# The S5 recurrence as one stage in four chunks: rotated inputs, a hardware scan, and GpSimd beside VectorE

## What is computed

```python
def s5_mixer(x, w_in, lam_re, lam_im, log_dt, b_re, b_im, c_re, c_im, d_skip, w_glu):
    ...
    u = (x @ w_in).astype(f32)
    ...
    a_bar = jnp.exp(lam * dt)
    b_bar = ((a_bar - 1.0) / lam)[..., None] * lax.complex(b_re.astype(f32), b_im.astype(f32))
    ...
        bu = jnp.einsum('gpc,btgc->btgp', b_bar, u_c.astype(jnp.complex64))
        _, hs = lax.associative_scan(binop, (jnp.broadcast_to(a_bar, bu.shape), bu), axis=1)
        hs = hs + a_pow[None] * h[:, None]
        y = jnp.einsum('gcp,btgp->btgc', c, hs).real
    ...
    y = jnp.moveaxis(ys, 0, 1).reshape(bsz, seq, D_MODEL) + d_skip.astype(f32) * u
    hid = jax.nn.gelu(y.astype(x.dtype), approximate=False)
    val, gate = jnp.split(hid @ w_glu, 2, axis=-1)
    return val * jax.nn.sigmoid(gate)
```

## Time and profile before

| | us |
|---|---|
| median of 3 runs | 2594.73 |
| lowest, highest | 2594.63, 2598.16 |
| span of the profiled execution, first to last instruction | 2590.5 |
| `s5_u`, from 836.3 to 886.3 | 50.0 |
| `s5_tables` to `s5_gelu`, from 886.3 to 981.0 | 94.7 |
| `s5_glu`, half clock at its start | 982.0 to 988.8 |

### The profile page before, as it was taken

The page is one execution under the profiler, slowest core; times in us unless marked ns, Lnnn a source line. Parts: engine busy times, 40 slices in busy tenths (PEclk is TensorE's granted clock), DMA queues, the critical chain, the costliest instruction groups (busy, mean ns, idle before and its releaser), DMA issues. The chain is left out here.

```text
span 2590.5 us, 41313 instructions
## 1 busy us (share of the span) xinstructions
PE 2477.6 (96%) x15961; PEld 2036.9 (79%) x15961; DVE 1739.2 (67%) x2869; ACT 1051.9 (41%) x1561; POOL 589.9 (23%) x447
## 2 busy tenths in 40 slices
PE   8998999999999989899999999998999999999998
PEld 6788887788887768899999999886776576767566
DVE  6945656467676784576666767676687567487667
ACT  4443233321212333355555555533344443344453
POOL 2404321430230020052333432440024001024001
PEclk9999999999999999999999999999999999999999
DMA  4321002346654252267776777853221211332121
GB/s 155 98 83 35 2 3 65 124 156 237 212 182 148 76 166 84 91 219 229 254 240 224 252 236 231 271 184 125 86 74 60 76 66 57 109 94 70 33 82 65
DMA packets 259968, 339.98 MB, mean 131 GB/s; under 512 B 24928, under 2 KB 217952, under 8 KB 259232
## 3 DMA queue, kind: packets, MB, share of 16 engines
q1 hardware_dynamic: 251840, 315.52, 37.6%
q0 software_dynamic: 4512, 15.99, 1.8%
q10 hardware_dynamic: 3456, 6.29, 0.8%
HBM read 318.63 MB, written 16.52 MB: 129 GB/s over the span
## 5 line engine op out<-in xcount | busy, mean ns | idle before, releaser
L3020 PE MATMUL ps<-x_feat_r,moe_w_hi 128*128 128x384 f32 x1408 | 405.1, 361 | 0.6 <-DVE x_feat_r L3132 0.6
L2545 DVE TENSOR_TENSOR moe_w_lo<-ring,moe_w_hi 128x2048 fp32r<-128x2048 f32 x144 | 316.1, 2196 | 126.8 <-ACT moe_w_hi L2540 126.6
L3023 PE MATMUL ps<-x_feat_r,moe_w_lo 128*128 128x192 f32 x1408 | 354.0, 251 | 0.0
L2540 ACT ACTIVATE moe_w_hi<-ring 128x2048 fp32r<-128x2048 f32 x144 | 254.8, 1770 | 93.5 <-PE ps L263 76.2
L3023 PEld LDWEIGHTS ps<-x_feat_r,moe_w_lo 128*128 128x128 f32 x1408 | 269.2, 191 | 0.3
L3020 PEld LDWEIGHTS ps<-x_feat_r,moe_w_hi 128*128 128x128 f32 x1408 | 264.3, 188 | 1.7 <-issue 1.4
L267 PE MATMUL ps<-x_free_r,ring_r 128*128 128x512 f32 x496 | 195.6, 394 | 0.0
L266 PE MATMUL ps<-ring_r,x_feat_r 128*128 128x256 f32 (+2 forms) x576 | 185.1, 321 | 0.0
L263 PE MATMUL ps<-x_feat_r,ffn_w_hi 128*128 128x512 f32 x352 | 139.3, 396 | 1.2 <-DVE ffn_w_lo L2488 1.2
L267 PE MATMUL ps<-x_feat_r,ffn_w_lo 128*128 128x512 f32 x352 | 139.4, 396 | 0.0
L266 PE MATMUL ps<-x_free_r,ffn_w_hi 128*128 128x512 f32 x352 | 138.5, 393 | 0.0
(11 more groups left out here) (661 smaller groups left out, 6407.1 us busy)
## 6 DMA issues: line engine op xcount, KB each, us to landing
ring<-in_moe_w SPq DMA_DIRECT2D x120, 1024.0 KB, 5.5
ring<-in_w_in SPq DMA_DIRECT2D x32, 1024.0 KB, 5.3
ring<-in_ffn_w SPq DMA_DIRECT2D x30, 1024.0 KB, 7.4
ring<-in_ada_t SPq DMA_DIRECT2D x48, 512.0 KB, 4.3
ring<-in_gdn_w_in SPq DMA_DIRECT2D x12, 1024.0 KB, 6.0
ring<-in_moe_w SPq DMA_DIRECT2D x24, 512.0 KB, 3.8
ring<-in_s_w_glu SPq DMA_DIRECT2D x8, 1024.0 KB, 5.6
ring<-in_w_out SPq DMA_DIRECT2D x8, 1024.0 KB, 6.2
```

What stands on the lines that cost most here:

```text
L2540: self.prog.nc.scalar.activation(self.flat(self.hi, j % SPLITS, j), self.raw(j), ACT.Copy).then_inc(self.hi_done, 1)
L2545: self.prog.nc.vector.tensor_tensor(self.flat(self.lo, j % SPLITS, j), self.raw(j), self.flat(self.hi, j % SPLITS, j).bitcast(F32), ALU.su ...
L3020: mm = nc.tensor.matmul(out, wh[:, k, cs], both[:, k, :], start=(k == 0), stop=False)
L3023: mm = nc.tensor.matmul(out[:, 0:SLOTS], wl[:, k, cs], xg[0][:, k, :], start=False, stop=(k == KD - 1))
```

## The change

Names first. `SC` = 4 chunks of `SQ` = 8 pairs. `S5Room` lays out the buffers: `u_ring` keeps only three feature blocks of u; `rot` holds cosine and sine of the angle of the pole's power for 63 steps, `decay` its magnitude.

- In `s5_u` GpSimd fills `rot` by doubling and `decay` by a broadcast copy (`rotations`): 36 products and sums, six for each of 32, 64, 128, 256, 512 and 992 elements in a partition. VectorE's own list there is the same as before.
- The four stages after it become one, `s5_core`. E stays in PSUM. For each chunk VectorE turns E by the angle (reading PSUM), runs `tensor_tensor_scan` with the real `decay` on the real and the imaginary part, multiplies by the cosine, and adds what GpSimd has made meanwhile: the two products by the sine (`cross`).
- The lags take b_bar widened to 32 columns (`lag_w`, which GpSimd fills), one matmul for both groups of a pair. The skip term is added to the lags (`add_skip`, GpSimd). `within` and `states` add up in the same PSUM banks, so VectorE's addition (L2366) and the skip operation (L2405) go.
- SyncE lays out each `mix` in 16 DMAs, in place of 8. After them it loads the four tiles of `s5_glu`, each when its chunk has been read.
- Of `keep_busy`, 14 matmuls stay in `s5_core`; before there were 16 in `s5_scan` and 18 in `s5_gelu`.

```diff
+def rotations(nc, link, s5, room):
+    tt = nc.gpsimd.tensor_tensor
+    rot, turn = room.rot, room.turn
+    nc.gpsimd.memset(rot[:, 0, :, 0], 1.0)
+    nc.gpsimd.memset(rot[:, 1, :, 0], 0.0)
+    for part in range(2):
+        nc.gpsimd.tensor_copy(rot[:, part, :, 1], s5.pole[:, 1 + part, :])
+    link(nc.gpsimd.tensor_copy(room.decay, s5.pole[:, 0, :].unsqueeze(2).to_broadcast([P, PAIRS, NJ])))
+    link(nc.gpsimd.memset(room.decay[:, :, 0], 0.0))
+    n = 1
+    while n < NJ - 1:
+        m = min(n, NJ - 1 - n)
+        shape = [P, PAIRS, m]
+        re, im = (rot[:, part, :, 1:m + 1] for part in range(2))
+        top_re, top_im = (rot[:, part, :, n:n + 1].to_broadcast(shape) for part in range(2))
+        t = [x[:, :, 0:m] for x in turn]
+        tt(t[0], re, top_re, ALU.mult)
+        tt(t[1], im, top_im, ALU.mult)
+        tt(t[2], re, top_im, ALU.mult)
+        link(tt(t[3], im, top_re, ALU.mult))
+        tt(rot[:, 0, :, n + 1:n + m + 1], t[0], t[1], ALU.subtract)
+        link(tt(rot[:, 1, :, n + 1:n + m + 1], t[2], t[3], ALU.add))
+        n += m
...
+        def u_feat(f):
+            return room.u_ring[:, f % room.U_RING]
...
+        @st.gpsimd
+        def _(pool):
+            rotations(nc, linker(pool, pool_link), s5, room)
...
+            turn_tables(0)
+            turn_tables(1)
+            inputs(0)
+            turn_tables(2)
+            turn_tables(3)
+            lags(0)
+            lags(1)
+            inputs(1)
+            lags(2)
+            lags(3)
+            within(0)
+            states(0)
+            inputs(2)
+            lags(4)
+            lags(5)
+            turn_back(0)
+            within(1)
+            states(1)
+            inputs(3)
+            lags(6)
+            lags(7)
+            turn_back(1)
+            within(2)
+            states(2)
+            turn_back(2)
+            within(3)
+            states(3)
+            pe.wait_ge(e_read, SC)
+            keep_busy(prog, E_BANK, 4)
+            turn_back(3)
+            keep_busy(prog, E_BANK, 10)
...
+            def scan(b):
+                e, t, h = room.e, room.t, room.h[b % 2]
+                shape = [P, 2, SQ, NJ]
+                cos, sin = (rot[:, part, chunk(b), :] for part in range(2))
+                dve.wait_ge(e_ready, b + 1)
+                raw = ps[:, E_BANK:E_BANK + 2, :].rearrange("p r (q j) -> p r q j", j=NJ)
+                tt(e, raw, cos.unsqueeze(1).to_broadcast(shape), ALU.mult)
+                tt(t[:, 0], raw[:, 1], sin, ALU.mult)
+                m = tt(t[:, 1], raw[:, 0], sin, ALU.mult)
+                m.then_inc(e_read, 1)
+                dve.wait_ge(e_read, b + 1)
+                tt(e[:, 0], e[:, 0], t[:, 0], ALU.add)
+                link(tt(e[:, 1], e[:, 1], t[:, 1], ALU.subtract))
+                decay = room.decay[:, chunk(b), :].rearrange("p q j -> p (q j)")
+                for r in range(2):
+                    m = nc.vector.tensor_tensor_scan(t[:, r].rearrange("p q j -> p (q j)"), decay,
+                                                     e[:, r].rearrange("p q j -> p (q j)"), 0.0, ALU.mult, ALU.add)
+                m.then_inc(scanned, 1)
+                dve.wait_ge(scanned, b + 1)
+                link(tt(e, t, cos.unsqueeze(1).to_broadcast(shape), ALU.mult))
+                late, early = slice(1, NJ), slice(0, NJ - 1)
+                dve.wait_ge(h_crossed, b + 1)
+                tt(h[:, 0, :, late], e[:, 0, :, early], h[:, 0, :, late], ALU.subtract)
+                link(tt(h[:, 1, :, late], e[:, 1, :, early], h[:, 1, :, late], ALU.add))
+                dve.sem_inc(h_ready, 1)
...
+            def cross(b):
+                if b >= 2:
+                    pool.wait_ge(y_ready, 2 * (b - 2) + 2)
+                pool.wait_ge(scanned, b + 1)
+                late, early = slice(1, NJ), slice(0, NJ - 1)
+                for r in range(2):
+                    m = nc.gpsimd.tensor_tensor(room.h[b % 2][:, r, :, late], room.t[:, 1 - r, :, early],
+                                                rot[:, 1, chunk(b), early], ALU.mult)
+                m.then_inc(h_crossed, 1)
+                pool.wait_ge(h_crossed, b + 1)
+            for b in range(SC):
+                zero(b)
+                add_skip(2 * b)
+                add_skip(2 * b + 1)
+                cross(b)
...
+        @st.sync
+        def _(sp):
+            sp.wait_ge(prog.u_last_stored, 16)
+            load_turned(prog, sp, u_blk, KD - 1)
             for s in range(NS):
...
+                sp.wait_ge(turned, min(8 + 4 * (s // 2), len(jobs)))
+                for r, dst in enumerate((q_re, q_im)):
+                    sp.dma_start(dst[:, quad(s), :, :], prog.q_dram[:, r, quad(s)]).then_inc(q_landed[s], 16)
+            for b in range(SC):
+                sp.wait_ge(zeroed, b + 1)
+                sp.wait_ge(skip_added, 2 * b + 2)
+                for i in range(STEP):
+                    n = (STEP - i) * GC
                     for gp in range(2):
...
+                        at = LR * b + GC * gp
+                        sp.dma_start(mix[b][i * GC:(i + 1) * GC, :, gp, i * GC:], room.lag[at:at + GC, :, 0:n]
+                                     ).then_inc(placed[b], 16)
+            for b in range(SC):
+                sp.wait_ge(y_ready, 2 * b + 2)
+                W.load(sp, W.issued)
+                W.issued += 1
...
-            for i in range(1, BLOCK):
-                y, out = h[:, :, i, :], h[:, :, i + 1, :] if i + 1 < BLOCK else total
-                tt(t0, y, one_re, ALU.mult)
-                tt(t1[:, :, RE], y[:, :, IM], one_im[:, :, RE], ALU.mult)
-                link(tt(t1[:, :, IM], y[:, :, RE], one_im[:, :, IM], ALU.mult))
-                link(tt(t0, t0, e[:, :, i, :], ALU.add))
-                link(tt(out, t0, t1, ALU.add))
...
```

More of the change, by code:

```diff
@@ L1708 @@
 PI_IN = 3.1415925
-GSTEP = 8
+SC = 4
+SQ = PAIRS // SC
+QUAD = SQ // 2
+LR = 2 * GC
 def reduce_angle(nc, link, x, tmp, shift=0.0):
@@ new lines, in inputs @@
+            def inputs(b):
+                for i in range(4 * b, 4 * b + 4):
+                    copied(pe, i)
+                if b:
+                    pe.wait_ge(e_read, b)
+                pe.wait_ge(prog.u_landed[b], 2 * 16 * STEP)
+                for r in range(2):
+                    for n in range(SQ):
+                        q = b * SQ + n
+                        for gp in range(2):
+                            m = nc.tensor.matmul(ps[TOKENS[gp], E_BANK + r, n * NJ:(n + 1) * NJ],
+                                                 into[r][:, q, TOKENS[gp]], u_blk[:, PAIRS * gp + q, :], start=True, stop=True)
+                m.then_inc(e_ready, 1)
@@ new lines, in within @@
+            def within(b):
+                pe.wait_ge(placed[b], 32 * STEP)
+                if b == 0:
+                    for i in range(len(jobs)):
+                        if bank_of(i) in (Y_BANK, Y_BANK + 1):
+                            copied(pe, i)
+                else:
+                    pe.wait_ge(y_copied, 2 * b)
+                for n in range(SQ):
+                    for gp in range(2):
+                        nc.tensor.matmul(ps[TOKENS[gp], Y_BANK + n // QUAD, n % QUAD * P:(n % QUAD + 1) * P],
+                                         u_blk[:, PAIRS * gp + b * SQ + n, :], mix[b][:, n, gp, :],
+                                         start=(n % QUAD == 0), stop=False)
@@ new lines, in states @@
+            def states(b):
+                pe.wait_ge(h_ready, b + 1)
+                for s in range(2):
+                    for n in range(s * QUAD, (s + 1) * QUAD):
+                        q = b * SQ + n
+                        for r, x in enumerate((q_re, q_im)):
+                            for gp in range(2):
+                                rows = TOKENS[gp]
+                                m = nc.tensor.matmul(ps[rows, Y_BANK + s, n % QUAD * P:(n % QUAD + 1) * P],
+                                                     room.h[b % 2][rows, r, n, :], flat_steps(x[rows, q, 1:STEP + 1, :]),
+                                                     start=False, stop=(n % QUAD == QUAD - 1 and r == 1))
+                    m.then_inc(y_ready, 1)
@@ L2315, in _ @@
+            scan(1)
+            scan(2)
+            split_lo(0)
+            scan(3)
+            for b in range(1, SC):
+                split_lo(b)
         @st.gpsimd
```

587 lines of the change are left out of this document (244 added, 343 removed).

## The result

The changed kernel takes 2601.83 us (median of 6 runs, 2598.21 to 2602.51), the kernel before 2594.68 (6 runs) in the same comparison: a ratio of 1.0026 (95% interval 1.0015 to 1.0036), slower by some 7 us. A second group of runs gave 1.0029 (1.0017 to 1.0041). The forecast was no visible change, 1.9 us faster. All ratios in this document leave out single runs in a slower state of the chip.

The account below looks back on a forecast made before the run. The core was taken as bound by a chain of tables, VectorE's recurrence, states and Gelu. Projection +14.9, core -13.9, `s5_glu` -2.9 give -1.9 us: median 2592.8 us, no visible change (0.45), range 2581 to 2605.

Parts of the forecast that it names:

- The price of GpSimd on VectorE: Projection stage: GpSimd's operations slow VectorE by 20.5 us together, so the stage ends 14.9 us later.
- Rival 4: Projection: GpSimd and VectorE exclude each other for the whole operation length; 27.2 us, +6.7, 2599.5 us; chance 0.13.
- The step on the last split: Projection: last split some 12 us late, TensorE's blocks 6 and 7 copied out by 896, so TensorE does not set the end.
- To the first `within`: C + 24.1: C is the core's start; SyncE's loads and first layout take 20.0 us from the first load, with 0.3 to start.
- The layout DMA: Core, chunk 3's layout on SyncE: 16 DMAs at 0.48 us each with gap, 7.6 us, landing 2.0.
- rival 3: Core: layout binds; DMAs cost 0.81 us each, a layout 13.0, +10.3, 2603.1 us; chance 0.13.
- The clock: Core: three longer TensorE idles, at the entry and ahead of `within(0)` and `within(3)`, cost 7 us in all through half clock.
- the forecast of 2.9 us: Start of `s5_glu`: keep-busy matmuls ending with the core keep TensorE's clock up, 2.9 us less.
- VectorE is hidden: Core: VectorE's 11.6 us a chunk, scans at 1.4 each, lie beside other work; no cost up to 3.9 us a scan.
- the trade that the prediction saw: Core gains 13.9 us, projection stage ahead of it loses 14.9: +1.0 at the core's end.

Follow-up runs that it names:

- Run 2: Changed kernel with VectorE's last weight split after 24 of its 48 table products, not 30: ratio 1.0020 to the kernel before.
- Runs 4 and 7: Changed kernel, half of each layout's DMAs issued by ScalarE: 1.0020; first two layouts only, with tables of pairs 16 to 31 loaded behind them: 1.0002.
- run 1: Changed kernel without GpSimd's 36 turned-angle operations, two fills instead (output not the reference's): ratio 0.9965 to the kernel before.

## Why the prediction was wrong, point by point

**The price of GpSimd on VectorE was right.** The forecast was 20.5 us. Measured, from VectorE's starts, less 0.68 us a product and 2.29 for a split: six operations of 992 elements cost 10.5 (11.4 forecast), six of 512 5.9 (5.1), six of 256 2.0 (1.8), the small ones 1.7 (1.6). VectorE's last table ends 0.6 us behind the forecast, 0.4 of it a later start of the stage. Rival 4, exclusion for the whole length, had 27.2. The Trainium skill (SBUF — State Buffer, "SBUF: two separate sides") has that rule. The trace agrees in kind: beside large operations the engines take turns (VectorE's product takes 2.38 us beside GpSimd's of 2.34). It does not agree that all of a GpSimd operation is lost to VectorE: 992 elements cost it 1.75 us each, not some 2.3, and the small ones 0.1. Here the measurement decides; why a part of each GpSimd operation costs VectorE nothing, no row shows.

**The step on the last split failed (+3.2 us: 2.6 for the split, 0.6 for VectorE's later end).** The prediction's "the last split (868.0 before) comes some 12 us late, blocks 6 and 7 wait for it at 873.6, end near 891 ... copied out by 896" is about what an even spread of the loss over the 48 products gives (20.5 x 30 / 48). But GpSimd's list ends at 887, so nearly all of it falls ahead of the split, with the large operations next to it: it ended at 889.1 in place of 868.0, 21 us late. So TensorE, and not VectorE, set the end of the stage. Its last two blocks start at 889.3 at half clock, and the copy of the last ends at 903.9, 2.6 us behind VectorE. Run 2 moved the split ahead of the large operations, and the stage ended with VectorE, 2.6 us shorter.

**"To the first `within`: C + 24.1" failed (+5.0 us).** The 20.0 us from the first table load were taken from before "with the same loads in front of the same layout". It was not the same layout: its first chunk took 8 DMAs before and takes 16 now, though the prediction itself counts 16 for chunk 3. From the first of them to the last start it was 8.25 us (912.71 to 920.96) and is 10.97 (920.61 to 931.58), 2.7 more, of which the loads ahead gave 0.3 back; the landing took 1.9 us both times. So 2.4 us come from the issues. Runs 4 and 7 show the limit right behind this one, the tables' 4.6 MB on the DMA engines: with the issues halved the first product came at C + 28.4, and only with half of the tables behind the layout as well at C + 23.8. The other part, 2.6 us, is the last block of u: its loads could only start when ScalarE's store had landed (903.93 to 906.31, 1.6 us later than taken), a term that stood in no line of the sum, and one of them was slow (1.0 us).

**The layout DMA was mis-sized (+3.4 us with the handovers around it).** The prediction took 0.48 us, by the number of pieces; measured are 0.64 between starts for every length of piece, and one of 1.3 to 1.6 in each layout: 10.95 us and not 7.6. For chunk 3 it is 12.1 us from the first issue to the landing (961.36 to 973.47) where 7.6 + 2.0 stood, 2.5 more; the rest is that this layout also started later behind its lags, 2.1 us and not 1.3. The median of L2313 said 0.62 and was the right row. This is rival 3, in its place but milder: not 0.81, and SyncE waited 8.2 us for the lags.

**The clock cost 5.2 us and not 7.** Half clock came behind the waits of 8.4 and 4.8 us, and not at the core's entry: `s5_u`'s late blocks kept TensorE at work until 902.8, and its idle time at the border was 1.9 us. In the next stage the forecast of 2.9 us stood against 2.8.

**VectorE is hidden, as said.** Two scans take 2.34 to 2.42 us, about 1.2 each (1.4 taken), and TensorE waits nowhere for `states`' inputs. The Trainium skill (DVE: opcode table, instruction layouts, handler registers and perf-mode slots, "Datapath and trigger behaviour") gives half throughput, by which the estimate was 1.2: the trace agrees.

Together 3.2 + 5.0 + 3.4 - 1.8 = 9.8 us, and with 0.2 for the rest the core's end at 992.0 against 982.0. With 0.1 less in `s5_glu` the forecast of -1.9 becomes +8.2 in the profile; the times say +7. So the trade that the prediction saw (a gain in the core given back a stage earlier) is there, but both sides of it were mis-sized the same way, towards faster: the loss in `s5_u` is 3 us larger and the gain in the core 7 us smaller. That the core would gain held in kind: run 1 takes GpSimd's work out and is at -9.1 us.

## What to carry to other kernels

Work given to an idle GpSimd was not free here, where VectorE has two SBUF inputs: 36 operations cost VectorE 21 us and would have taken it 17. Put such work where VectorE waits for something else, and ask which of VectorE's results others wait for behind the slowed stretch. For a small transfer on the chain, count both its issues and the bytes that are already under way ahead of it: here the two limits lay 0.6 us apart at the first chunk, and curing the issues alone gained no more than that there.

## What the runs showed of the hardware that was not expected

- A layout DMA costs its queue 0.64 us whether its pieces have 512 or 64 bytes (from 920.61 to 931.58: 16 starts, with one longer step of 1.45 us), a load of u with 256-byte pieces 0.47.
- Beside VectorE's products a GpSimd operation of 32 elements takes 0.70 to 0.76 us (839.79 to 841.90), as long as one of 256 in the earlier trace rows; VectorE lost only about 0.1 us for each.
